# First 16 stick-breaking score chunks of prompt attention run inside the keys stage, gate products on VectorE

## What is computed

```python
def stick_breaking_block(q, k, v, q_pos, k_pos):
    z = jnp.einsum('bqhd,bkhd->bhqk', q, k).astype(jnp.float32) * (SB_HEAD_DIM ** -0.5)
    causal = k_pos[None, :] < q_pos[:, None]
    log_beta = jax.nn.log_sigmoid(z)
    log_rem = jnp.where(causal, log_beta - z, 0.0)
    tail = lax.cumsum(log_rem, axis=3, reverse=True) - log_rem
    w = jnp.where(causal, jnp.exp(log_beta + tail), 0.0)
    return jnp.einsum('bhqk,bkhd->bqhd', w.astype(v.dtype), v)
...
    kv = (all_ckv @ w_ukv).reshape(b, tk, MLA_HEADS, MLA_NOPE_DIM + MLA_V_DIM)
    k_nope, mla_v = kv[..., :MLA_NOPE_DIM], kv[..., MLA_NOPE_DIM:]
    sb_o = sweep_query_blocks(stick_breaking_block, (sb_q,), (all_sb_k, all_sb_v), pos, k_pos)
    mla_o = sweep_query_blocks(mla_block, (q_nope, q_rope), (k_nope, all_krope, mla_v), pos, k_pos)
    mixed = jnp.concatenate([sb_o.reshape(b, t, SB_WIDTH) * jax.nn.silu(sb_g),
                             mla_o.reshape(b, t, MLA_WIDTH) * jax.nn.silu(mla_g)], axis=-1)
```

## Time and profile before

| | us |
|---|---|
| median of 3 runs | 2401.71 (2399.45 to 2404.94) |
| the profiled execution | 2401.62 |
| its span, first to last instruction | 2399.80 |
| keys stage and what follows up to the first step of attention | about 795 to 1053 |
| 8 heads of 80 steps | 1053 to 1980 |
| end of the last head up to the tail | 1980 to 1997 |

### The profile page before, as it was taken

The page is one execution under the profiler, slowest core; times in us unless marked ns, Lnnn a source line. Parts: engine busy times, 40 slices in busy tenths (PEclk is TensorE's granted clock), DMA queues, the critical chain, the costliest instruction groups (busy, mean ns, idle before and its releaser), DMA issues. The chain is left out here.

```text
span 2399.8 us, 39253 instructions
## 1 busy us (share of the span) xinstructions
PE 2171.5 (90%) x11972; PEld 1805.5 (75%) x11972; DVE 1344.6 (56%) x2777; ACT 1276.2 (53%) x2614; POOL 899.1 (37%) x927
## 2 busy tenths in 40 slices
PE   6999998999989799779898999999999992999998
PEld 1888886999988477658686868686777781887886
DVE  3232232300028333278788888888888863676683
ACT  2232232311113333257878888888888883567553
POOL 0000000000000000164949494858585744656673
PEclk9999999999999999969999999999999995999999
DMA  7433332322347699944343434343433214676772
GB/s 277 139 96 104 96 116 83 128 73 73 121 149 198 218 315 317 275 101 89 76 92 72 100 71 103 70 103 67 99 77 89 62 32 144 192 224 183 217 215 86
DMA packets 297066, 320.37 MB, mean 133 GB/s; under 512 B 88706, under 2 KB 221853, under 8 KB 291955
## 3 DMA queue, kind: packets, MB, share of 16 engines
q1 hardware_dynamic: 292130, 302.26, 44.9%
q10 hardware_dynamic: 2880, 9.05, 1.0%
q0 software_dynamic: 1904, 7.41, 0.8%
HBM read 199.36 MB, written 110.90 MB: 129 GB/s over the span
## 5 line engine op out<-in xcount | busy, mean ns | idle before, releaser
L1446 ACT ACTIVATE pa_whi<-banks 128x512 fp32r<-128x512 f32 (+3 forms) x640 | 341.0, 536 | 111.4 <-PE banks L1682 96.4
L1682 PE MATMUL banks<-ident,pa_p 128*128 128x128 f32 x2176 | 345.6, 274 | 0.0
L1611 POOL TENSOR_TENSOR pa_wlo<-pa_whole,pa_whi 128x512 fp32r<-128x512 f32 (+2 forms) x240 | 277.1, 1174 | 126.7 <-ACT pa_whole L1451 126.7
L1682 PEld LDWEIGHTS banks<-ident,pa_p 128*128 128x128 f32 x2176 | 270.8, 141 | 58.5 <-issue 1.3
L1669 PE MATMUL banks<-pa_khi,pa_qst 128*128 128x512 f32 (+3 forms) x640 | 258.1, 403 | 62.1 <-DVE pa_p L1504 51.6
L1643 PE MATMUL banks<-pa_whi,pa_vst 128*128 128x512 f32 (+3 forms) x640 | 281.8, 440 | 17.6 <-POOL pa_wlo L1611 17.6
L1504 DVE TENSOR_TENSOR_SCAN pa_p<-banks,pa_p,pa_zero 128x512 f32<-128x512 f32 x192 | 246.3, 1283 | 65.3 <-ACT banks L1406 58.0
L1481 DVE TENSOR_TENSOR pa_wlo<-banks,pa_whi 128x512 fp32r<-128x512 f32 (+3 forms) x400 | 234.4, 586 | 28.7 <-ACT pa_whi L1446 27.8
L699 POOL DMA_DIRECT2D gate_ada<-in_ada_w_dram x2 | 1.8, 886 | 641.5 <-DVE qu_wlo L755 641.5
L1670 PE MATMUL banks<-pa_klo,pa_qst 128*128 128x512 f32 (+3 forms) x640 | 238.5, 373 | 0.0
L1643 PE MATMUL banks<-pa_wlo,pa_vst 128*128 128x512 f32 (+3 forms) x640 | 234.2, 366 | 0.0
(11 more groups left out here) (257 smaller groups left out, 5149.9 us busy)
## 6 DMA issues: line engine op xcount, KB each, us to landing
scratch_sb_kT<-ke_kT SPq DMA_DIRECT2D x12, 1024.0 KB, 9.0
scratch_mla_kT<-ke_nT SPq DMA_DIRECT2D x12, 1024.0 KB, 5.2
scratch_mla_v<-ke_v SPq DMA_DIRECT2D x12, 1024.0 KB, 5.4
scratch_gatesT<-co_gates SPq DMA_DIRECT2D x12, 704.0 KB, 11.3
ada<-in_ada_w_dram SPq DMA_DIRECT2D x4, 2048.0 KB, 11.6
pr_x<-in_x_prompt_dram SPq DMA_DIRECT2D x16, 512.0 KB, 18.0
scratch_hT<-pr_hT SPq DMA_DIRECT2D x16, 512.0 KB, 5.0
ke_k<-in_cache_sb_k_dram SPq DMA_DIRECT2D x8, 1024.0 KB, 7.7
```

The source lines that it names most:

```text
L1446: act.activation(whi[:, t % NW, q0:], bank, ACT.Copy).then_inc(hi_done, 1)
L1611: pool.tensor_tensor(wlo[:, t % NW, q0:], whole[:, t % 4, q0:], raw(whi[:, t % NW, q0:]), ALU.subtract).then_inc(pool_lo, 1)
L1682: y = pe.transpose(ps[:, NS + t % NTB, x * P:(x + 1) * P], probs[g][x][:, i * P:(i + 1) * P], s["ident"][:])
```

## The change

Five edits, which hang together:

- In the keys stage `nT` and `v` each use one bank (4 and 6) and take turns, slot by slot. Banks 5 and 7 are free, and in groups 10 and 11 two chunks of head 0 stand behind each slot: chunks 0 to 15, with sigmoid and scan. The weights of these chunks, the causal mask and a zero lie in memory that the gate's matmuls had used before (`gate_ada`).
- `load_first_head` is issued behind the stores of group 3 rather than ahead of those of group 10, with the causal mask ahead of it.
- The constants are rounded by POOL at the start of the keys stage, stored to memory, and loaded rounded by attention. POOL's five casts at the start of attention fall away.
- Attention starts with chunks 16 to 19 (READY = 16). `finish` on ACT becomes `take` on DVE: one product of the bank and the gates (both halves), at the end of the step, behind the chunk's scan. POOL only adds. The add stands one step earlier (ADD = 3). The gates of a group are loaded behind the move of the group before.
- `on_pool` leaves out t = 60, 61 and 62: DVE makes their `pa_wlo`, and ACT makes no second copy.

```diff
@@ keys stage
+        N_BANK, V_BANK, LEAD_BANKS = 4, 6, (5, 7)
+        def lead_after(p, b, slot):
+            first = 8 * b + 2 * slot
+            return range(first, first + 2) if isinstance(p, int) and p == 5 else ()
...
                 def back(p, b, n):
-                    if isinstance(p, int) and 2 * p + b == 10:
-                        load_first_head()
...
+                    if isinstance(p, int) and 2 * p + b == 3:
+                        load_first_head()
...
-                        act.activation(nT[:, b, m, 0:n], ps[:, 4 + m % 2, 0:n], ACT.Copy).then_inc(n_ev, 1)
+                        act.activation(nT[:, b, m, 0:n], ps[:, N_BANK, 0:n], ACT.Copy).then_inc(n_ev, 1)
+                        for x in lead_after(p, b, m):
+                            _, _, _, width, bank = lead_of(x)
+                            act.wait_ge(lead_scores, x + 1)
+                            act.activation(ps[:, bank, 0:width], ps[:, bank, 0:width], ACT.Sigmoid, scale=-SB_SCALE)\
+                               .then_inc(lead_sig, 1)
...
+                        for x in lead_after(p, b, m):
+                            _, q, first_key, width, bank = lead_of(x)
...
+                            if x >= 2:
+                                pe.wait_ge(lead_scan, x - 1)
+                            keys = slice(first_key, first_key + width)
+                            pe.matmul(ps[:, bank, 0:width], qst[:, q], khi[:, keys], start=True, stop=False)
+                            pe.matmul(ps[:, bank, 0:width], qst[:, q], klo[:, keys], start=False, stop=True)\
+                              .then_inc(lead_scores, 1)
@@ prompt attention
+    READY = 16
-    ADD = 4
+    ADD = 3
...
-            return (t + LEAD) % HEAD < JOB and t % 4 != 3
+            return 4 <= (t + LEAD) % HEAD < JOB and t % 4 != 3
...
-                act.activation(out[:, n % 2, :], ps[:, 6 + n % 2, :], ACT.Copy).then_inc(taken, 1)
...
+                def take(h, n):
+                    dve.wait_ge(mixed, NW + HEAD * h + upto(n))
+                    dve.wait_ge(stored[n % 2], 16 * (G * h + n // 2))
+                    dve.wait_ge(gates_loaded, 32 * (GROUPS * h + n + 1))
+                    dve.tensor_tensor(out[:, n % 2, :], ps[:, 6 + n % 2, :], gates[:], ALU.mult).then_inc(taken, 1)
...
                     pool.wait_ge(moved[n % 2], 16 * (G * h + n // 2 + 1))
-                    pool.tensor_tensor(out[0:HD, n % 2, :], out[0:HD, n % 2, :], half[:], ALU.add).then_inc(added, 1)
-                    wait_apart(pool, added, GROUPS * h + n + 1, passed)
-                    pool.wait_ge(gates_loaded, 16 * (GROUPS * h + n + 1))
-                    pool.tensor_tensor(out[0:HD, n % 2, :], out[0:HD, n % 2, :], gates[:], ALU.mult).then_inc(fin_done, 1)
+                    pool.tensor_tensor(out[0:HD, n % 2, :], out[0:HD, n % 2, :], half[:], ALU.add).then_inc(fin_done, 1)
```

More of the change, by code:

```diff
@@ L1 @@
+import itertools
 from contextlib import ExitStack
@@ L1335, in load_v, with load_gates @@
                         sp.dma_start(step_v[EVEN:P, 0], v[EVEN - 1:P - 1]).then_inc(v_loaded, 16)
+                def load_gates(h, n):
+                    rows = bass.ds(h * HD + (n // G) * WIDTH, HD)
+                    cols = slice(size_of(n) * CH, (size_of(n) + 1) * CH)
+                    for i in range(2):
+                        sp.dma_start(gates[i * HD:(i + 1) * HD, :], d["gatesT"][rows, cols]).then_inc(gates_loaded, 16)
                 def move(h, n):
@@ L1451, in step @@
                         act.activation(whole[:, t % 4, q0:], bank, ACT.Copy).then_inc(whole_done, 1)
-                    n = ends_at(t)
-                    if n is not None and not is_none(past(h, n)):
-                        finish(past(h, n), n)
                     if last and t + LEAD in (HEAD, HEAD + 1):
@@ L1502, in chunk @@
                             end = first_key + width
-                            given, start = zero[:].to_broadcast([P, width]), tile[:, end:end + 1]
+                            given, start = zero.to_broadcast([P, width]), tile[:, end:end + 1]
                         dve.tensor_tensor_scan(tile[:, first_key:first_key + width][:, ::-1], scored[:, ::-1], given, start,
@@ L1539, in step @@
                     chunk(*chunk_at(h, t, last))
-                for m in range(LEAD):
+                    if n is not None and not is_none(past(h, n)):
+                        take(past(h, n), n)
+                for m in range(READY, LEAD):
                     chunk(0, m)
-                dve.wait_ge(const_done, 1)
                 steps_in_turn(dve, step)
@@ L1547, in _ @@
                     finish(HEADS - 1, n)
+                    take(HEADS - 1, n)
             @block.gpsimd
@@ L2407, in build_program @@
             s["first"] = [first.enter_context(nc.sbuf_tensor(f"pa_{n}0", [P, T_PROMPT], F32R)) for n in ("khi", "klo", "qst")]
-            with ExitStack() as modulation:
-                s["ada"] = modulation.enter_context(nc.sbuf_tensor("gate_ada", [P, 2, DC, 512], F32))
-                queries_phase(nc, outer, d, s, ps)
-                keys_phase(nc, outer, d, s, ps)
+            ahead = first.enter_context(nc.sbuf_tensor("gate_ada", [P, 2 * DC * 512], F32))
+            s["ada"] = ahead[:].rearrange("p (i c n) -> p i c n", i=2, c=DC)
+            ends = list(itertools.accumulate([0] + [(12 + i + 1) * P for i in range(4)] + [512, 1]))
+            *s["first_probs"], s["causal"], s["zero"] = (ahead[:, a:b] for a, b in zip(ends, ends[1:]))
+            queries_phase(nc, outer, d, s, ps)
+            keys_phase(nc, outer, d, s, ps)
             prompt_attention_phase(nc, outer, d, s, ps)
```

150 lines of the change are left out of this document (91 added, 59 removed).

## The result

| | before | after |
|---|---|---|
| median, us | 2404.7 (2399.45 to 2406.85) | 2416.06 (2414.99 to 2416.59) |
| span of the profiled execution | 2399.78 | 2413.13 |
| TensorE's mean granted clock | 0.964 | 0.958 |

The change makes the kernel slower: 1.0047 of the time before, 95% interval 1.0035 to 1.0059, some 11 us. The forecast was 2381, range 2360 to 2398, with 0.08 on slower.

What follows compares the result with a forecast made beforehand. PE was taken as busiest, with POOL and the sigmoid-scan-chunk chain holding steps 60 to 19. From 2401.6 us: keys stage and start -0.7, heads -14.2, end -6, giving 2380.7, said as 2381; own range 2368 to 2393, stated range 2360 to 2398.

Steps and rivals of the forecast that it cites:

- Steps 0 to 19: In each head, POOL loses three products and PE's wait at step 13 goes: -2.1 us a head, -14.7 in 7 heads.
- Keys stage, the new stall: At group 6, PE waits for loads queued behind the first head's, then runs at half clock: +11 us, bounds +7 and +16.
- The rest of the keys stage: Old end stall gone -7.3 us, chunks 0 to 15 on PE +7.0, sigmoid table +0.3, one `nT` bank +1.0.
- Start of attention: Up to the first mix in step 4: mix 14.9 us sooner, held by POOL's splits, half clock +2.2: -12.7 us.
- Steps 60 to 79: In each head, ACT's relief gains 0 by scan 3, then -0.2 us a head in steps 64 to 79, -1.5 in all.
- Steps 20 to 59: In each head, four more products on busy DVE, late out of the scans: +0.3 us a head, +2 in all.
- The end: From the last head's step 60, serial POOL loses three `pa_wlo` and four products: -6 us, bounds -3 and -9.
- VectorE as the pace: Steps 60 to 19: seven more DVE instructions a head delay the scans in full, 33 us in 7 heads, 2414; chance 0.08.
- The port's rival: In the heads, work moved from POOL to VectorE gains nothing (shared read port); 14.2 us lost, 2395; chance 0.07.

Runs made afterwards that it cites:

- poolqueue: The changed kernel with the first head's loads and the mask issued by POOL's queue in place of SP's; 2414.82 us, ratio to before 1.0045.
- vlastfirst: The changed kernel with `vlast` loaded as the first DMA of prompt attention, ahead of rotary keys, own tile and masks; 2409.24 us, ratio to before 1.0027.
- vlate: The changed kernel with the first head's four value loads issued behind the stores of group 10; 2409.14 us, ratio to before 1.0032.
- turn22: The changed kernel with the loop's turn at step 22 of a head in place of step 12; 2419.56 us, ratio to before 1.0067.

## Why the prediction was wrong, step by step

- **Steps 0 to 19, -2.1 a head: wrong, and the step that turned the sign.** Forecast -14.7; heads 1 to 6 came to +1.4 each and head 7 to -1.0, +7.7 in all, 22 us off. Two readings failed. The 2.4 us between head 0 and a later head were put down to POOL's products; but head 0 also has no turn of the loop (its steps 13 to 19 take 8.97 for 11.07, just the 2.1 counted, without either). And the 1.28 us at step 13 were taken as a wait that goes with POOL's work; the releaser named is the one that came last, and under it lay ACT's and DVE's turn. PE's idle time in steps 13 to 19 stayed (2.18 us before, 2.12 after), and what turned the sign is the half clock behind the one long gap. What POOL's relief is worth by itself in these steps is 1.25 a head (10.20 to 8.95 without turns), 60% of what I took.
- **Keys stage, the new stall, +11 (bounds 7 and 16): right place, too small, and for another reason.** Fronts 5 to 7 cost 17.7 us. I had counted the time of SP's issues, 15.65 us less 5.7 of slack; they took 22.5 less 8.0, and poolqueue shows that taking them off SP changes the wait by 1.8 of 14.5 us. The term should have been the engines' time: what was moved was 3.2 MB, 17.4 us of all 16 engines, out of the end of the stage, where little else was due, into a stretch with 8% of the engines' time free.
- **The rest of the keys stage, +1.0: about right.** 18.9 less 17.7 leaves +1.2, nearly all of it ahead of group 2's front, where executions of the same code differ by 2. The chunks cost 3.1 us in group 10, for half of the 7.0; what they cost in group 11 no run tells apart from what ends the stage.
- **Start of attention, -12.7: nearly right** at -10.8. POOL's splits are what the first mix waits for, at the forecast length (16.9 for 17.0); the 2 us missing are `vlast`'s landing, 7.0 us for 5, within the bounds of 2 and 7.7. No row showed the lower bound; vlastfirst has 1.6.
- **Steps 60 to 79, -0.2 a head:** +0.2. ACT's relief gave 0.87 in steps 60 to 63, which the count by hand had given back by step 63 already; it was given back in steps 64 to 79, 1.06. **Steps 20 to 59, +0.3:** nothing. **The end, -6:** -3.8 in head 7's last steps and -2.3 behind, but the second is no more than what it varies by, so that the sum is met is in part luck.
- **The rivals.** VectorE as the pace (2414) gave nearly the time that was measured, by chance, and is not what happened: without turns, with the same seven instructions on DVE, steps 13 to 19 are the shortest of all, and in steps 60 to 79 the three `pa_wlo` on DVE cost 0.27 us a head. The port's rival has nothing for it either, as POOL's relief came out in full in head 7. The rival that was missing is a second wait at the same step, under the one removed.

By the sum: 2380.7 forecast and 2414.99 measured in the profiled execution differ by 34: steps 0 to 19 22, the keys stage 7, the other steps 1, the start 2, and 2 that lie ahead of the keys stage.

## What to carry to other kernels

Before a stall is credited to the engine that it names, look at the same step in an iteration that lacks one of the suspects (the first, the last, the one behind the loop), and look there at all suspects, since a first iteration lacks more than one thing. Where DMA engines are busy to nine tenths, count what a load takes of the engines' time, from the same load elsewhere in the trace, and not its place in a queue; at the end of a stage, where little else was due, vlate's late load cost nothing. And a chunk of work moved ahead gains only what the next thing in front of its consumer leaves: here POOL's splits, in an order that cost 7 us more than it had to.

## What the runs showed of the hardware

- A loop's turn on ACT and DVE, with bodies of about 400 instructions, costs 2.4 to 3.1 us, with a transfer of instructions behind each branch; on ACT with 43, DVE with 52 and POOL with 142 to 180 instructions it costs 0.16 to 0.34, on PE with 826 it costs 0.02. Written out for 8 heads the same code showed no cost of its own: steps 20 to 59 take 56.25 us for 56.41.
- One gap of 1.8 to 2.1 us on PE between busy stretches was followed by 3.4 us at 1.2 GHz in six heads of six of the changed kernel; gaps of 1.28, 0.40 and 0.28 us with work between them left the clock at 2.4 GHz. In turn22 gaps of 2.50 and 2.64 us left it there too, so one gap's length alone doesn't decide.
- A DMA of 4 KB landed 1.6 us behind its issue as the first of a stage, and 7.0 us as the fifth, behind 1.3 MB.
- Keys and queries, loaded into 64 rows each in pieces of 8 KB, kept the DMA engines full at 224 GB/s; values in pieces of 256 bytes at 145; loads and stores in pieces of 2 KB at 408.
